# Three experts instead of two with fixed places in a decoder step's expert loop, and a new order of passes

## The chip, the cores and the metric

The kernel runs on one core of a Trainium2 chip. The metric is the device time of one execution in microseconds. TensorE (PE) multiplies, VectorE (DVE), ScalarE (ACT) and GpSimd (POOL) do the rest, and SyncE (SP) issues most of the transfers; all work from their own instruction queues and meet at semaphores. The core's transfers share 16 DMA engines.

## The reference, cut to what matters

One decoder layer for 512 prompt rows and 64 sample rows of width 1024, all in float32: a state space branch and an attention branch, merged and projected by `w_o`, then 16 experts of which each row uses two, then a gated embedding and a final norm. The change touches the experts and the loads around `w_o`:

```python
def hier_moe(h, w_rg, b_rg, w_re, b_re, w_gate, w_up, w_down):
    ...
        glog = (hf @ w_rg + b_rg).astype(f32)
        gsel = jnp.argmax(glog, axis=-1)
        ...
        top_v, top_i = lax.top_k(elog, TOP_K_INNER)
        wts = jax.nn.softmax(top_v, axis=-1) * gw
        eid = gsel[:, None] * EXPERTS_PER_GROUP + top_i
        comb = jnp.einsum('cke,ck->ce', jax.nn.one_hot(eid, N_EXPERTS, dtype=f32), wts)
        a = jnp.einsum('cd,edf->cef', hf, w_gate)
        b = jnp.einsum('cd,edf->cef', hf, w_up)
        act = jax.nn.silu(a) * b * comb[..., None].astype(hf.dtype)
        return jnp.einsum('cef,efd->cd', act, w_down)
...
        x = x + mix
        x = x + hier_moe(rms_norm(x, norm2_g[l]), ...)
        x = x + jax.nn.sigmoid(x @ w_ple_gate[l]) * (p_l @ w_ple[l])
```

The 576 rows make 1152 choices. A gate or up matrix of one expert is 1024 x 256 and a down matrix 256 x 1024, 1 MiB each, 48 MiB for all.

## The kernel before, in words

After the attention the two branches' products fill `merged`, and `w_o` (loaded as two halves, `wo0` for output columns 0 to 511 and `wo1` for 512 to 1023) multiplies it. `second_norm_steps` is the hand-written order of TensorE's steps from there: products with `w_o` ("m", pair of tiles, number), transposes ("xT"), router products ("rt", "rb"), and the products of the embedding ("pp"). `w_o_product` (L1640 on) says which half each product reads: the first, number 1 of pair 0, reads `wo0`. The last reader of `wo1` is product 7 of pair 1, the last of `wo0` is product 4 of pair 1, which comes later.

Then the experts are computed by gathered rows. A pass has 128 rows: rows of `h2_dram` (the normed rows, stored in five pieces) are gathered by a list, turned on TensorE, multiplied by gate and up (`gate_up`, L1766, or `gate_up_of_two`, L1779), activated, turned and multiplied by down (`down`, L1803, or `down_of_two`, L1812), and stored to `ye_dram`. TensorE's order in the loop (L1850 on) is gate and up of pass n, turn of pass n-1, rows of pass n+1, down of pass n-1.

An expert stands at one of 16 columns. The experts are sorted by their number of rows, and `RANK_OF_COLUMN` says which rank goes to which column. `COLUMNS_OF_PASS` says which columns a pass computes: a pass of one column has 128 slots for it, a pass of two gives 96 (or 64) to the first and 32 (or 64) to the second. Columns 12, 13 and 14 are small and are split over two neighbouring passes, so their weights stay for two passes. Experts 0 and 1 have columns 0 and 1 whatever their counts, so their weights can be loaded before the router is done. The rows of an expert that has more than its column's slots would be computed in a second round of the whole loop.

Weights are loaded in the order `LOADED`. Load number l of gate and up goes to slot l mod 4: slots 0 and 1 are `wgu`, slots 2 and 3 are ring buffers 1 and 2, in which before that the halves of `w_o` lie. Load number l of down goes to slot (l + 2) mod 3, of which two are in `merged`. On SyncE `gate_up_weights(l)` waits until the last pass that reads load l - 4 has done its gate and up products, and `down_weights(l)` until the last pass that reads the load before in the same slot has done its down products (`LAST_PASS`, `down_before`). SyncE does this in one fixed order, written out at L965 to L991. The gathers are issued by GpSimd and the stores by ScalarE, from queues of their own.

## Time and profile before

| | us |
|---|---|
| median of three runs | 799.75 |
| lowest and highest | 797.71, 799.83 |
| the profiled execution | 797.28 |
| its span | 795.5 |

Busy in that span: TensorE 762.2 us (96%), VectorE 379.9 (48%), ScalarE 204.9 (26%), GpSimd 106.8 (13%). The chain of work that ended last is TensorE for 80% of the span and DMA for 8%, and within the DMA part the loads of down matrices are the largest. The output projection runs from 485 to 550 us, the experts from 566 to 716, the gated embedding and the last norm from there to the end. The rows further down are of four kinds: windows (busy time of each engine in a stretch, then the granted clock, the busy share of the DMA engines and GB/s), waits (who waited for whom), the chain in order of time, and timelines of single engines.

### The profile page before, as it was taken

How to read it: one execution, taken by the hardware profiler on the slowest of the kernel's cores; microseconds unless marked ns; L12 is line 12 of the kernel's file. 1: busy time of each engine (PE TensorE's matmuls, PEld its weight loads, DVE VectorE, ACT ScalarE, POOL GpSimd, SP SyncE). 2: the span in 40 equal slices, each digit the busy share in tenths (PEclk: the TensorE clock that was granted, in tenths of full speed). 3: DMA queues.
4: the chain of work that ended last, by engine and by line, in shares of the span. 5: the costliest groups of instructions: out<-in, count | busy, mean ns of one | idle time of the engine just before them, and what ended most of it. 6: DMA issues, size and time to landing. Idle time of an engine off the chain costs nothing.

```text
span 795.5 us, 12983 instructions
## 1 busy us (share of the span) xinstructions
PE 762.2 (96%) x5070; PEld 494.9 (62%) x5070; DVE 379.9 (48%) x850; ACT 204.9 (26%) x485; POOL 106.8 (13%) x160
## 2 busy tenths in 40 slices
PE   8999999999999999889999999999999999998995
PEld 5455588777778788555566775445556564654442
DVE  3269523997232323766624378434732212214865
ACT  3011213112223354654523200134111111123223
POOL 3000006000000311334500100011111101015002
PEclk9999999999999999999999999999999999999998
DMA  9640493841440499200030279003799999996002
GB/s 324 160 126 0 112 278 139 99 133 57 140 97 17 139 233 266 94 1 1 1 120 2 96 216 384 1 14 128 282 407 409 416 418 416 417 373 211 17 14 106
DMA packets 81287, 136.50 MB, mean 172 GB/s; under 512 B 33926, under 2 KB 57546, under 8 KB 77010
## 3 DMA queue, kind: packets, MB, share of 16 engines
q1 hardware_dynamic: 64700, 110.17, 41.7%
q0 software_dynamic: 3728, 13.38, 4.9%
q10 hardware_dynamic: 12798, 12.12, 4.6%
q8 instruction: 41, 0.67, 0.3%
q14 instruction: 20, 0.16, 0.1%
HBM read 116.55 MB, written 21.19 MB: 173 GB/s over the span
## 4 chain that ended last, share of the span: by engine, by line
PE 80%; DMA 8%; DVE 6%; issue 2%; ACT 2%; POOL 1%; DVEq 0%; SPq 0%; POOLq 0%; ACTq 0%
PE ps L1215 29%; PE ps L1300 10%; PE ps L1656 6%; PE ps L1904 5%; PE ps L1788 4%; PE ps L1222 3%; PE ps L1776 3%; DMA merged<-in_w_exp_down 3%; DMA w_slot<-in_w_exp_down 2%; PE ps L1441 2%; PE ps L1820 2%; PE ps L1491 2%; PE ps L1537 2%; PE ps L1518 2%; DMA wgu<-expert_rows,pos_i 1%
## 5 line engine op out<-in xcount | busy, mean ns | idle before, releaser
L1215 PE MATMUL ps<-w_slot,hT 128*128 128x396 f32 (+1 forms) x192 | 71.1, 529 | 0.6 <-DMA w_slot<-in_w_in 0.4
L1215 PE MATMUL ps<-hT,w_slot 128*128 128x288 f32 x256 | 63.1, 407 | 0.0
L1215 PEld LDWEIGHTS ps<-hT,w_slot 128*128 128x128 f32 x256 | 48.3, 190 | 13.9 <-issue 0.8
L1215 PEld LDWEIGHTS ps<-w_slot,hT 128*128 128x128 f32 x192 | 36.1, 190 | 32.5 <-issue 13.4
L2987 DVE SCALAR_TENSOR_TENSOR th<-th,ps 128x256 f32<-128x256 f32 x12 | 5.1, 421 | 103.2 <-ACT th L2248 103.2
L1788 PE MATMUL ps<-w_slot,hT 128*32 128x256 f32 x544 | 49.7, 380 | 0.0
L1300 PE MATMUL ps<-hT,w_slot 128*128 128x288 f32 x144 | 37.3, 407 | 0.0
L1215 PE MATMUL ps<-qg,w_slot 128*128 128x288 f32 x128 | 33.7, 408 | 0.0
L1788 PEld LDWEIGHTS ps<-w_slot,hT 128*32 128x32 f32 x544 | 26.3, 110 | 10.0 <-issue 2.3
L2728 DVE TENSOR_REDUCE nm_p<-ps 128x2 f32<-128x256 f32 (+3 forms) x32 | 25.0, 819 | 15.6 <-PE ps L1491 15.5
L1300 PEld LDWEIGHTS ps<-hT,w_slot 128*128 128x128 f32 x144 | 27.3, 190 | 7.6 <-issue 0.2
L1088 POOL TENSOR_TENSOR hT<-hT,w_p 128x512 f32<-128x512 f32 (+3 forms) x11 | 25.1, 2284 | 50.6 <-DVE w_p L2360 50.6
L1215 PE MATMUL ps<-onsaT,w_slot 128*128 128x288 f32 x128 | 31.2, 406 | 0.0
L1776 PE MATMUL ps<-wgu,hT 128*128 128x256 f32 x128 | 28.9, 382 | 0.9 <-DVE hT L2360 0.9
L2148 ACT ACTIVATE hT<-ps,nm_p 128x128 f32<-128x128 f32 (+3 forms) x44 | 22.6, 524 | 26.1 <-DVE nm_p L2728 19.0
L1215 PEld LDWEIGHTS ps<-onsaT,w_slot 128*128 128x128 f32 x128 | 24.3, 190 | 6.7
L1788 PE MATMUL ps<-wgu,hT 128*32 128x256 f32 x352 | 28.3, 379 | 0.0
L1999 ACT ACTIVATE hT<-ps 128x512 f32<-128x512 f32 (+1 forms) x14 | 7.2, 553 | 81.8 <-PE ps L1699 71.0
L1776 PEld LDWEIGHTS ps<-wgu,hT 128*128 128x128 f32 x128 | 23.9, 190 | 6.7 <-issue 2.5
L2360 DVE TENSOR_TENSOR qg<-qg,ps 128x288 f32<-128x288 f32 x18 | 8.2, 455 | 39.6 <-PE ps L1300 39.5
L1215 PEld LDWEIGHTS ps<-qg,w_slot 128*128 128x128 f32 x128 | 23.2, 190 | 5.4
L1820 PE MATMUL ps<-merged,actT 128*32 128x512 f32 x160 | 25.4, 595 | 0.5 <-ACT actT L2252 0.5
(508 smaller groups left out, 1416.5 us busy)
## 6 DMA issues: line engine op xcount, KB each, us to landing
merged<-in_w_exp_down SPq DMA_DIRECT2D x10, 1024.0 KB, 15.9
w_slot<-in_w_in SPq DMA_DIRECT2D x8, 1024.0 KB, 7.7
wgu<-in_w_exp_gate SPq DMA_DIRECT2D x8, 1024.0 KB, 12.1
wgu<-in_w_exp_up SPq DMA_DIRECT2D x8, 1024.0 KB, 14.1
w_slot<-in_w_exp_gate SPq DMA_DIRECT2D x8, 1024.0 KB
w_slot<-in_w_exp_up SPq DMA_DIRECT2D x8, 1024.0 KB
w_slot<-in_w_exp_down SPq DMA_DIRECT2D x6, 1024.0 KB
expert_rows<-onsaT ACTq DMA_DIRECT2D x12, 512.0 KB, 8.2
```

Source lines behind the costliest of these rows:

```text
L1088: pool.tensor_tensor(p4, p4, w_p[:, i].rearrange("p a b -> p (a b)").unsqueeze(2).broadcast_to([P, 4, n]), ALU.mult).then_inc(pr_scaled, 1)
L1215: ins = pe.matmul(out, a, b, start=(n == 0), stop=(n == len(pairs) - 1))
L1222: ins = pe.matmul(out[64 * c:64 * c + 64, 0:n], a, b[c], start=(k == 0), stop=(k == len(pairs) - 1))
L1300: ins = pe.matmul(o[:, 0:HALF], weights[:, k], rows[:, k], start=(first and k == 0), stop=(k == 3), skip_group_check=True)
L1441: ins = pe.matmul(ps[:, 7, 0:NBLK], w1(k)[:, n], kvct[:, k, n % CS, n // CS:n // CS + NBLK], start=(n == 0), stop=(n == CL - 1))
L1656: ins = pe.matmul(o, rows[:, k], weights[:, k], start=(k == 0 and i in (1, 2, 5)), stop=(k == 3), skip_group_check=True)
L1776: ins = pe.matmul(ps[:, 2 + u, FF * w:FF * w + FF], hgT[:, u, k], w0[:, w, k], start=(k == 0), stop=(k == KD - 1))
L1788: ins = pe.matmul(ps[g:g + 32, 2 + u, FF * w:FF * w + FF], hgT[:, u, k, g:g + 32], gate_up_slot(l)[:, w, k], start=(k == 0), stop=(k == KD ...
L1820: ins = pe.matmul(ps[g:g + 32, 4 + c, :], actT[:, u, f, g:g + 32], down_slot(l)[:, f, 512 * c:512 * c + 512], start=(f == 0), stop=(f == 1))
L1904: ins = pe.matmul(o, rows[:, k], weights[:, k], start=(k == 0 and i in (1, 2, 5)), stop=(k == 3), skip_group_check=True)
L2148: ins = act.activation(probs[i % PBUFS][:, (2 * c + kh) * n:(2 * c + kh) * n + n], ps[:, 2 * (at % 2) + kh, 0:n], ACT.Exp, bias=nm_p[:, at ...
L2728: dve.tensor_reduce(nm_p[:, at], ps[:, 2 * (at % 2):2 * (at % 2) + 2, 0:n], axis=X, op=ALU.max, negate=True).then_inc(pr_max, 1)
```

## The change

Expert 2 gets a fixed column too. `RANK_OF_COLUMN`, `COLUMNS_OF_PASS` and `LOADED` are new: passes 0 to 2 compute experts 0, 1 and 2 alone, and the seven paired passes are 3, 4, 6, 7, 8, 9 and 10 (before 1, 2, 4, 5, 7, 8 and 10). The halves of `w_o` change ring buffers, so that `wo1`, which is done with first, lies where gate and up number 2 go; these two loads are issued right after router step ("rb", 1). SyncE's order in the loop is rewritten for the new passes.

```diff
+PINNED = 3
-COLUMNS_OF_PASS = [[0], [1, 12], [2, 12], [3], [4, 13], [5, 13], [6], [7, 14], [8, 14], [9], [10, 15], [11]]
+COLUMNS_OF_PASS = [[0], [1], [2], [3, 12], [4, 12], [5], [6, 13], [7, 13], [8, 15], [9, 14], [10, 14], [11]]
...
-LOADED = [0, 1, 12, 2, 3, 4, 13, 5, 6, 7, 14, 8, 9, 10, 15, 11]
+LOADED = [0, 1, 2, 3, 12, 4, 5, 6, 13, 7, 8, 15, 9, 14, 10, 11]
...
-           ("so", ("ab", KD - 1, 1)), ("no", ("bb", KD - 1, 1)), ("wo0", AFTER_W_O), ("wo1", AFTER_W_O),
+           ("so", ("ab", KD - 1, 1)), ("no", ("bb", KD - 1, 1)), ("wo1", AFTER_W_O), ("wo0", AFTER_W_O),
...
-            load_weights("wo0")
+            load_weights("wo1")
...
-            load_weights("wo1")
+            load_weights("wo0")
...
+            sp.wait_ge(pe_done, PLAN.done(("rb", 1)))
+            load_gate_up(2, 2)
             sp.wait_ge(pe_done, PLAN.done(AFTER_W_O))
             sp.wait_ge(h2_out[0], 16 * 3)
             sp.wait_ge(h2_out[1], 16 * 2)
             load_down(1, 1)
             sp.wait_ge(order_made, 1)
-            at_column = {0: 0, 1: 1}
+            at_column = {i: i for i in range(PINNED)}
...
-            for l in range(2, NX):
+            for l in range(PINNED, NX):
                 read_column(l)
                 load_gate_up(l, expert(l))
             load_down(2, expert(2))
...
                 gate_up_weights(5)
                 down_weights(3)
                 gate_up_weights(6)
+                down_weights(4)
                 gate_up_weights(7)
-                down_weights(4)
+                down_weights(5)
                 gate_up_weights(8)
-                down_weights(5)
+                gate_up_weights(9)
                 down_weights(6)
-                gate_up_weights(9)
+                gate_up_weights(10)
                 down_weights(7)
-                gate_up_weights(10)
+                down_weights(8)
                 gate_up_weights(11)
-                down_weights(8)
+                down_weights(9)
                 gate_up_weights(12)
-                down_weights(9)
+                gate_up_weights(13)
                 down_weights(10)
-                gate_up_weights(13)
-                down_weights(11)
                 gate_up_weights(14)
                 gate_up_weights(15)
+                down_weights(11)
                 down_weights(12)
...
-            for at, cap in ((slice(0, 1), 128), (slice(1, 3), 96), (slice(3, 4), 128), (slice(4, 6), 96), (slice(6, 7), 128),
-                            (slice(7, 9), 96), (slice(9, 10), 128), (slice(10, 11), 64), (slice(11, 12), 128), (slice(12, 16), 64)):
+            for at, cap in ((slice(0, 3), 128), (slice(3, 5), 96), (slice(5, 6), 128), (slice(6, 8), 96), (slice(8, 9), 64),
+                            (slice(9, 11), 96), (slice(11, 12), 128), (slice(12, 16), 64)):
                 pool.memset(cap_at[:, at], float(cap))
...
-            for e in range(2):
+            for e in range(PINNED):
                 pool.memset(first_at[:, e:e + 1], float(2 ** (21 - e)))
...
-                    pe.matmul(out[96:P, 1 + h:8 + h:3], ident[:, 32 * h:32 * h + 32], by_column[:, 12:15], start=True, stop=True)
-                return pe.matmul(out[64:P, 10:11], ident[:, 0:64], by_column[:, 15:16], start=True, stop=True)
+                    pe.matmul(out[96:P, 3 + h:10 + h:3], ident[:, 32 * h:32 * h + 32], by_column[:, 12:15], start=True, stop=True)
+                return pe.matmul(out[64:P, 8:9], ident[:, 0:64], by_column[:, 15:16], start=True, stop=True)
```

The slots of the columns change with it: 128 for columns 0, 1, 2 (fixed experts), 5 and 11, 64 for columns 8 and 12 to 15, 96 for the rest. The two busiest other experts have 128 slots, the third busiest 96.

SyncE's queue from the rows of the embedding to the first expert that the sort decides, before (`w_slot0` to `w_slot2` are the ring buffers, `kv`, `merged` and `wgu` hold what their sources say; `order_i` is the sorted list of experts):

```order
L923 DMA kv<-in_p_prompt 128x4x256 [waits merged_made,outputs_written]
L924 DMA kv<-in_p_sample 64x256
L751 DMA w_slot0<-in_w_ple 128x2x1024 [waits pe_done]
L918 DMA w_slot0<-in_w_exp_down 128x2x1024
L928 DMA kv<-in_final_norm_g 128x1024 [waits pe_done]
L918 DMA merged<-in_w_exp_down 128x2x1024 [waits h2_written1,h2_written0,pe_done]
L941 TENSOR_LOAD order_i [waits rows_gathered0,order_made]
L941 ISA x2
L914 ISA
L914 DMA w_slot1<-in_w_exp_gate 128x2048
L914 DMA w_slot1<-in_w_exp_up 128x2048
L941 TENSOR_LOAD order_i
```

and after:

```order
L929 DMA kv<-in_final_norm_g 128x1024 [waits pe_done]
L915 DMA w_slot1<-in_w_exp_gate 128x2048 [waits pe_done]
L915 DMA w_slot1<-in_w_exp_up 128x2048
L919 DMA merged<-in_w_exp_down 128x2x1024 [waits h2_written1,h2_written0,pe_done]
L944 TENSOR_LOAD order_i [waits rows_gathered0,order_made]
L944 ISA x2
L915 ISA
L915 DMA w_slot2<-in_w_exp_gate 128x2048
L915 DMA w_slot2<-in_w_exp_up 128x2048
L919 DMA merged<-in_w_exp_down 128x2x1024
```

The loads into `w_slot1` have moved ahead of the wait for the stores of the normed rows and of the wait for the sort.

SyncE's queue late in the expert loop, before, from down number 11 (to `merged`) over gate and up 14 and 15 (to `w_slot1` and `w_slot2`) to down number 12 (to `w_slot0`):

```order
L918 DMA merged<-in_w_exp_down 128x2x1024 [waits down_done]
L955 REGISTER_ALU
L914 ISA [waits gate_up_done]
L914 DMA w_slot1<-in_w_exp_gate 128x2048
L914 DMA w_slot1<-in_w_exp_up 128x2048
L914 ISA [waits gate_up_done]
L914 DMA w_slot2<-in_w_exp_gate 128x2048
L914 DMA w_slot2<-in_w_exp_up 128x2048
L960 REGISTER_ALU
L918 DMA w_slot0<-in_w_exp_down 128x2x1024 [waits down_done]
L960 REGISTER_ALU
```

and after, from down number 10 (to `merged`) over gate and up 14 and 15 to down numbers 11 and 12:

```order
L919 DMA merged<-in_w_exp_down 128x2x1024 [waits down_done]
L958 REGISTER_ALU
L915 ISA [waits gate_up_done]
L915 DMA w_slot1<-in_w_exp_gate 128x2048
L915 DMA w_slot1<-in_w_exp_up 128x2048
L915 ISA [waits gate_up_done]
L915 DMA w_slot2<-in_w_exp_gate 128x2048
L915 DMA w_slot2<-in_w_exp_up 128x2048
L963 REGISTER_ALU
L919 DMA merged<-in_w_exp_down 128x2x1024 [waits down_done]
L919 DMA w_slot0<-in_w_exp_down 128x2x1024 [waits down_done]
L963 REGISTER_ALU
```

Down number 11 has moved behind gate and up 14 and 15.

## Rows read from the trace of the kernel before

**Rows 1.** The page: busy time by engine, and TensorE's clock, DMA and GB/s in slices.

```profile
PE 762.2 (96%) x5070; PEld 494.9 (62%) x5070; DVE 379.9 (48%) x850; ACT 204.9 (26%) x485; POOL 106.8 (13%) x160
...
PEclk9999999999999999999999999999999999999998
```

**Rows 2.** The expert stage in one window: busy us per engine, clock, DMA share, GB/s.

```profile
600.00:700.00 100.00, 98.06 (x1028) 58.91 (x1017) 16.32 (x32) 15.71 (x34) 6.88 (x12) 1.00 1.02 415
```

**Rows 3.** TensorE's timeline, passes 1, 4, 6 and 7: start us, us, instruction, [idle before <-releaser].

```profile
577.69 0.42 PE L1788 MATMUL ps<-wgu,hT 128*32 128x256 f32 x3
...
624.62 7.11 PE L1788 MATMUL ps<-w_slot,hT 128*32 128x256 f32 x128
...
636.47 7.17 PE L1776 MATMUL ps<-wgu,hT 128*128 128x256 f32 x32
...
648.13 0.39 PE L1788 MATMUL ps<-wgu,hT 128*32 128x256 f32 x3
...
657.73 3.70 PE L1215 MATMUL ps<-merged,actT 128*128 128x512 f32 x8 [1.27 <-DMA merged<-in_w_exp_down]
```

**Rows 4.** TensorE's waits from 560 to 740: us in total, times, longest.

```profile
PE ps L1924 <- DVE x L2360: 2.0, 1, 2.0
...
PE ps L1820 <- DMA merged<-in_w_exp_down: 0.6, 1, 0.6
```

**Rows 5.** The chain that ended last, in order of time: start us, us, what.

```profile
649.05 21.17 DMA merged<-in_w_exp_down
...
674.09 19.80 DMA w_slot<-in_w_exp_down
693.94 3.71 PE ps L1215 x8
...
698.30 7.17 DMA expert_rows<-onsaT
...
707.58 10.33 DMA wgu<-expert_rows,pos_i
...
720.20 1.25 PE ps L1924 x8
```

**Rows 6.** The issues of down loads (L918): issue to landing.

```profile
DMA to landing us min/median/max: 4.9/15.9/21.2
```

**Rows 7.** The second half of W_o: its landing, its issue, and TensorE's first product.

```profile
w_slot<-in_w_o SPq DMA_DIRECT2D x1, 2048.0 KB, 8.7
...
471.22 0.43 SPq L751 DMA_DIRECT2D w_slot<-in_w_o  x1
...
485.13 3.60 PE L1656 MATMUL ps<-w_slot,merged 128*128 128x512 f32 x8
```

**Rows 8.** Around the router: TensorE, a window, SyncE and GpSimd.

```profile
543.93 0.29 PE L1718 MATMUL ps<-groups_sum,actT 128*128 128x20 f32 x2
...
543.00:552.00 9.00, 8.67 (x62) 5.26 (x64) 3.95 (x8) 4.96 (x7) 1.84 (x5) 1.00 0.15 61
...
557.62 0.37 SPq L918 DMA_DIRECT2D merged<-in_w_exp_down  x1
...
546.73 0.61 POOL L1123 DMA_DIRECT2D h_rows<-hn  x1
...
560.89 1.06 POOL L1137 DMA_INDIRECT hT<-h_rows,idx  x1 [5.67 <-DVE idx L2360]
```

**Rows 9.** SyncE's waits around the router.

```profile
SPq L931 <- DMA h_rows<-hn: 17.1, 1, 17.1
```

**Rows 10.** TensorE's last product and windows of the end, columns as in rows 2.

```profile
782.02 3.60 PE L1904 MATMUL ps<-merged,hT 128*128 128x512 f32 x8
...
788.00:790.00 2.00, 0.00 (x0) 0.00 (x0) 1.97 (x3) 1.13 (x4) 0.20 (x1) 1.00 0.00 0
790.00:792.00 2.00, 0.00 (x0) 0.00 (x0) 1.00 (x2) 0.12 (x2) 1.15 (x3) 0.56 0.30 123
792.00:794.00 2.00, 0.00 (x0) 0.00 (x0) 0.97 (x2) 0.00 (x0) 0.00 (x0) 0.50 0.76 294
```

More of the change, by code:

```diff
@@ L61 @@
 MAXR = -(-ROWS // CAP)
-RANK_OF_COLUMN = [0, 1, 6, 2, 7, 8, 3, 9, 10, 4, 14, 5, 11, 12, 13, 15]
-COLUMNS_OF_PASS = [[0], [1, 12], [2, 12], [3], [4, 13], [5, 13], [6], [7, 14], [8, 14], [9], [10, 15], [11]]
+PINNED = 3
+RANK_OF_COLUMN = [0, 1, 2, 5, 6, 3, 7, 8, 14, 9, 10, 4, 11, 12, 13, 15]
+COLUMNS_OF_PASS = [[0], [1], [2], [3, 12], [4, 12], [5], [6, 13], [7, 13], [8, 15], [9, 14], [10, 14], [11]]
 NPASS = len(COLUMNS_OF_PASS)
 OF_PARITY = [-(-NPASS // 2), NPASS // 2]
-LOADED = [0, 1, 12, 2, 3, 4, 13, 5, 6, 7, 14, 8, 9, 10, 15, 11]
+LOADED = [0, 1, 2, 3, 12, 4, 5, 6, 13, 7, 8, 15, 9, 14, 10, 11]
 LAST_PASS = [max(n for n, columns in enumerate(COLUMNS_OF_PASS) if column in columns) for column in LOADED]
@@ L1102, in _ @@
             row_of(base_at[:, 0:NPASS], 0, CAP)
-            row_of(base_at[:, 12:15], CAP + 96, 3 * CAP)
-            pool.memset(base_at[:, 15:16], float(10 * CAP + 64))
-            for at, cap in ((slice(0, 1), 128), (slice(1, 3), 96), (slice(3, 4), 128), (slice(4, 6), 96), (slice(6, 7), 128),
-                            (slice(7, 9), 96), (slice(9, 10), 128), (slice(10, 11), 64), (slice(11, 12), 128), (slice(12, 16), 64)):
+            row_of(base_at[:, 12:15], 3 * CAP + 96, 3 * CAP)
+            pool.memset(base_at[:, 15:16], float(8 * CAP + 64))
+            for at, cap in ((slice(0, 3), 128), (slice(3, 5), 96), (slice(5, 6), 128), (slice(6, 8), 96), (slice(8, 9), 64),
+                            (slice(9, 11), 96), (slice(11, 12), 128), (slice(12, 16), 64)):
                 pool.memset(cap_at[:, at], float(cap))
@@ L1109, in _ @@
                 pool.memset(split_at[:, at], float(split))
-            for e in range(2):
+            for e in range(PINNED):
                 pool.memset(first_at[:, e:e + 1], float(2 ** (21 - e)))
-            row_of(first_at[:, 2:NE], NE - 3, -1)
-            for at in (slice(0, 2), slice(2, 3), slice(3, 4), slice(4, 6), slice(6, 7), slice(7, 9), slice(9, 10), slice(10, 11),
-                       slice(11, 12), slice(12, 15), slice(15, 16)):
+            row_of(first_at[:, PINNED:NE], NE - 1 - PINNED, -1)
+            for at in (slice(0, 3), slice(3, 5), slice(5, 6), slice(6, 8), slice(8, 9), slice(9, 11), slice(11, 12), slice(12, 15), slice(15, 16)):
                 row_of(rank_of[:, at], RANK_OF_COLUMN[at.start], 1)
```

## The prediction, made before the changed kernel ran

> **What bounds the kernel now.** I read the page's slices first, then the expert stage in windows, then who waits for whom, then the chain. TensorE has work in 96% of the span and its clock is granted in full until the last slice [rows 1]. So a change gains only where TensorE stands still, and loses wherever it makes it stand. In the expert stage (566 to 716 us) two things run side by side at nearly the same pace. From 600 to 700 us 415 GB/s move and the 16 DMA engines are full (share 1.02) [rows 2]. TensorE takes 11.74 us a pass: gate and up of pass 1 begin at 577.69, of pass 7 at 648.13, six passes later [rows 3]. A paired pass costs what a single one does (7.11 against 7.17 us for gate and up, 3.7 for down) [rows 3], so the new order of passes changes none of TensorE's own work: seven passes are paired before and after. TensorE waits for weights three times only: 1.27 us, 0.55 us and some 0.1 us, 1.9 us in all, each time for a down projection [rows 3, 4, 5]. The reader is to see in the chain how they come about: a down load issued at 649.05 lands 21.17 us later, one issued at 674.09 lands 19.80 us later, because all SyncE loads stand in one line [rows 5]. Unloaded, the same load lands in 4.9 us [rows 6]. So the margin of a load is the time from its issue to its use, and its issue is bound to the pass that frees its slot.
>
> **Part by part.**
>
> *W_o halves swapped.* The half that TensorE reads first (columns 0 to 511) now comes second. The second half is issued at 471.22 and takes 8.7 us [rows 7], so it is there at 479.9. Its first reader is the product at 485.13 [rows 7]: 5 us to spare, cost 0. Without that cover the whole projection would slip by what is missing.
>
> *Expert 2's gate and up (two loads, 2 MiB) behind the router product of tile 1.* The slot of the old second half is free once that product's row (TensorE, 543.93) is done. 2 MiB are 2.1 MB, 5.1 us at 415 GB/s; from 543 to 552 the engines move 61 GB/s, so there is room [rows 8]. Queued behind it on SyncE are the wait for the five stores of normed rows (17.1 us) and behind it the down load at 557.62 [rows 8, 9], 13 us later: free. Beside it runs the store issued at 546.73, which may land some 2 us late; the first gather at 560.89 waits for the list of rows, not for it [rows 8]. Cost 0 to 1 us, 0 taken. A load that had stood at 566.18, 2 MiB or 5.1 us of the line, is gone from the full stretch.
>
> *What the early load is worth.* At most the 1.9 us of waits: TensorE has no other wait for weights.
>
> *Tables.* GpSimd runs three small table writes fewer, on an engine that is ahead at this point. 0.
>
> *The order of passes.* This is the term that counts. A load of gate and up needs the slot of the load four before it, a down load that of three before it. I wrote down for each load the pass that frees its slot and the pass that reads it. Before, every down load has two passes between (slot free after down of pass n, read by down of pass n+2). After, two have one: number 11 (column 15, read in pass 8) takes the slot of number 8 (column 13), whose last reader is now pass 7; number 13 (column 14, read in pass 9) takes the slot of column 8, read in pass 8. Number 11 can be issued only when down of pass 7 ends, and down of pass 8 starts 11.74 - 3.5 = 8.2 us later, where the landings of before are 16 to 21 us. In front of it in the line stand gate and up 14 and 15, released together by gate and up of pass 8.
>
> Its landing: in the new order TensorE takes one expert a pass in passes 0 to 2, so loads run at one slot a pass and the line runs empty. Per pass 3 MiB of weights, 0.5 MiB gathered and 0.5 MiB written are 4.2 MB, 10.1 us of 11.74. It is empty for the last time when gate and up of pass 4 end, at 577.69 + 3 x 11.74 + 7.1 = 620.0, where two loads are released at once. From there to the end of number 11: gate and up of eight experts (8 to 15, 2 MiB each), six downs (6 to 11, 1 MiB), five gathers and five stores of 0.5 MiB, 27 MiB = 28.3 MB. At 415 GB/s [rows 2] that is 68.2 us. With 2.4 us from the last byte's turn to the landing (4.9 us [rows 6] less 2.5 us of transfer) it lands at 620.3 + 68.2 + 2.4 = 690.9, the 0.3 being SyncE's own step. The same count made for before, from 566.2 to number 12 (48.5 MiB, 122.5 us), gives 691.1 where the trace has 693.89 [rows 5]; scaled to 68 us that adds 1.5. I take 691.6, between. Down of pass 8 would start at 577.69 + 8 x 11.74 + 7.1 + 1.3 = 680.0. TensorE slips by 11.6 us, about 2 of them already in front of gate and up of pass 9 (number 13 of those, counted likewise, lands near 673.5, wanted at 671.6), the rest in front of down of pass 8. Against the 1.9 us of before: **+9.7 us**. Least case: only gate and up 14 and 15, the down and 1 MiB of row traffic stand in the line from 667.6 on, 6.3 MB or 15.2 us plus 2.4: 685.2, a slip of 5.2, +3.3 net. Most: an effective 405 GB/s, 693.5, +11.6 net.
>
> Number 13 is issued when down of pass 8 ends, near 695.2, into an empty line, lands by 700 to 703 and is wanted at 703.6: 0.
>
> *The clock.* TensorE stands still for 9 to 10 us there. The trace has one such stretch, its end: the last products start at 782.02 and end by 785.6; the clock is granted in full up to 790, 0.56 from 790 to 792 and 0.50 from there, the lower level of 1.2 GHz [rows 10]. So it falls within the stall. No row shows it coming back; the cost lies between 0 and a whole down at half speed, 3.5 us. I take the middle, **+1.7 us**.
> The Trainium skill (TensorE: Matmul & The Clock Gate, Part 1, on the HAM clock gate) says that the clock stays at the lower level at first when work resumes. By it the term is above zero; without any such effect the sum below would be 1.7 us less.
>
> *The tail.* Before, the store of pass 9's rows takes 7.17 us and the gather behind it 10.33 us, TensorE waits 2.0 us for tile 0 and starts at 720.20 [rows 4, 5]. In the new order the stall has let the line run down, so both land some 3 us earlier against TensorE, and the products that cover them end at 718.2: **-2.0 us** (0 to -2).
>
> Sum: +9.7 + 1.7 - 2.0 = **+9.4 us**. On the profiled run (797.28 us, span 795.5) 806.7; on the median of the runs, 799.75, 809.2. The profiled run is at the low end of the runs (797.71 to 799.83), so I take a value between, 808.5.
>
> **Rivals.**
> *A shorter stall.* If less stands in the line than I count, the net slip is 3.3 to 7 us, the clock stays or costs little, the tail gives 2: 801 to 805. For it: the line runs empty earlier. Against it: the same count fits before within 2.6 us.
> *No stall, the purpose reached.* The 1.9 us of waits and the 2.0 us of the tail go: 799.75 - 3.9 = 795.9. It needs number 11 to land within 8.2 us with 4 MiB in front of it; the smallest landing of an unloaded 1 MiB is 4.9 us, and 4 MiB are 10 us more.
> *A longer one.* The clock costs its full 3.5, number 13 comes late as well by 2 to 4 us, the tail gives nothing: 813 to 818.
> *A second round.* The fixed experts have 128 slots each, but the third busiest of the rest now has 96 instead of 128. Counting the router's choices on the reference's inputs (seed 0) gives 82, 80 and 100 rows for experts 0 to 2 and 113, 111, 90, 86, 69 and less for the rest: all fit, one round. With 97 rows in one place the whole loop would run again, some 12 x 11.74 = 141 us more.
>
> **How the numbers follow.** The forecast 0.74, a shorter stall 0.12, no stall 0.05, a longer one 0.08, a second round 0.01. The range of 802.5 to 814 holds the forecast with its bounds (net slip 7 to 11.6, clock 0 to 3.5, tail 0 to -2, on either base) and half of its two neighbours. About 0.3%, 2.4 us, is what a measurement of this kernel can tell from no change. Slower by more than that: 0.89; within it 0.06 (the lower edge of the short stall, a little of no stall); faster 0.05.
>
> **What would show it.** A wait of 8 to 10 us in front of the paired down product, between 680 and 693, for a down load whose slot is an expert's, and 1 to 3 us in front of gate and up one pass earlier; a granted clock below 1.00 there; idle DMA time between 575 and 620 where there was none; the loads of expert 2 between 544 and 552 and the first pass still at 569.7. I am wrong if that load lands before 684, if the line is not served in order, or if the first pass starts later than 571.

## The result, and the profile after

| | before | after |
|---|---|---|
| median, us | 798.88 (4 runs) | 809.46 (4 runs) |
| lowest and highest | 797.71, 799.83 | 808.96, 811.46 |
| the profiled execution, its span | 797.28, 795.5 | 809.38, 807.6 |

The ratio is 1.0138, 95% interval 1.0111 to 1.0165: slower by 10.6 us, inside the range and 1 us over the forecast. Medians and ratios in this document are of the fast runs, which leaves out one run of two_first_pg0 (1587 us) and three of the kernel before beside the experiments.

In the changed kernel all line numbers are two or three higher: `gate_up` is L1778, `gate_up_of_two` L1790, `down_of_two` L1822, the loads of gate and up L915, of down L919. TensorE's waits from 560 to 760 us, which answer to [rows 4]:

```profile
PE ps L1822 <- issue: 8.1, 1, 8.1
PE ps L1790 <- DMA wgu<-in_w_exp_up: 3.5, 1, 3.5
PE ps L1790 <- DMA w_slot<-in_w_exp_up: 1.2, 1, 1.2
```

Three waits in a row, 12.8 us, where there were three of 1.9 us together. The trace puts the longest down to "issue", that is, to nothing it can name; the place and the landing below tell what it is. TensorE's timeline around it (start us, us, instruction, [idle before <-releaser]), which answers to [rows 3]:

```profile
661.24 7.11 PE L1790 MATMUL ps<-w_slot,hT 128*32 128x256 f32 x128 [1.19 <-DMA w_slot<-in_w_exp_up]
...
676.68 7.59 PE L1790 MATMUL ps<-wgu,hT 128*32 128x256 f32 x128 [3.52 <-DMA wgu<-in_w_exp_up]
684.48 1.04 PE L1761 MATMUL ps<-ident,hT 128*128 128x128 f32 x8
693.58 6.30 PE L1822 MATMUL ps<-merged,actT 128*32 128x512 f32 x32 [8.06 <-issue]
...
719.59 3.64 PE L1822 MATMUL ps<-merged,actT 128*32 128x512 f32 x32 [0.46 <-ACT actT L2254]
```

The rows are gate and up of pass 8, gate and up of pass 9, the turn of the rows, down of pass 8, and down of pass 10, the last paired one. The down product of pass 8 waits 8.06 us, and its 32 matmuls then take 6.30 us where those of pass 10 take 3.64. SyncE's issues in the same stretch, for what it waited for:

```profile
668.61 0.33 SPq L915 DMA_DIRECT2D w_slot<-in_w_exp_gate  x1
669.04 0.38 SPq L915 DMA_DIRECT2D w_slot<-in_w_exp_up  x1
669.67 0.33 SPq L915 DMA_DIRECT2D w_slot<-in_w_exp_gate  x1
670.10 0.39 SPq L915 DMA_DIRECT2D w_slot<-in_w_exp_up  x1
673.34 0.38 SPq L919 DMA_DIRECT2D merged<-in_w_exp_down  x1
673.91 0.38 SPq L919 DMA_DIRECT2D w_slot<-in_w_exp_down  x1
700.05 0.92 SPq L919 DMA_DIRECT2D merged<-in_w_exp_down  x2
```

and, for the load issued at 673.34, its size and its time to landing:

```profile
merged<-in_w_exp_down SPq DMA_DIRECT2D x1, 1024.0 KB, 20.1
```

Down load 11 goes out at 673.34, behind 4 MiB, and is wanted at 685.52. It lands at about 693.5, and TensorE starts at 693.58: the same kind of landing as the 19.8 and 21.2 us of [rows 5], on a load that now has one pass of room and not two. After 673.91 nothing is issued for 26 us, because every further load waits for a product that waits for this one. Windows (busy us per engine, granted clock, DMA share, GB/s) show how much the line carries, and the clock:

```profile
580.00:600.00 20.00, 20.00 (x91) 15.35 (x90) 7.25 (x30) 2.93 (x7) 2.29 (x4) 1.00 0.97 366
600.00:620.00 20.00, 20.00 (x278) 10.84 (x276) 2.04 (x4) 2.62 (x6) 1.14 (x2) 1.00 1.00 361
620.00:640.00 20.00, 20.00 (x188) 12.39 (x188) 4.08 (x8) 3.71 (x8) 2.28 (x4) 1.00 1.00 391
...
688.00:690.00 2.00, 0.00 (x0) 0.00 (x0) 0.00 (x0) 0.00 (x0) 0.00 (x0) 0.68 0.99 401
690.00:692.00 2.00, 0.00 (x0) 0.00 (x0) 0.00 (x0) 0.00 (x0) 0.00 (x0) 0.50 1.03 414
...
696.00:698.00 2.00, 2.00 (x16) 0.65 (x12) 0.00 (x0) 0.60 (x1) 0.00 (x0) 0.50 0.00 0
698.00:700.00 2.00, 2.00 (x24) 0.65 (x19) 0.00 (x0) 0.07 (x1) 0.00 (x0) 0.76 0.00 0
700.00:702.00 2.00, 2.00 (x44) 1.26 (x40) 0.00 (x0) 0.53 (x1) 0.00 (x0) 1.00 0.42 37
```

The clock falls during the wait, stands at 0.50 (1.2 GHz) when work comes back at 693.6, and is full (2.4 GHz) again only from some point between 698 and 700. From 696 to 700 us nothing at all moves.

**Where the 12.1 us between the two spans are.** The times of a stretch have to be counted from a mark, since each execution loses a different amount before the experts: the first gate product starts at 569.71 in the trace of before and here at

```profile
570.34 5.45 PE L1778 MATMUL ps<-wgu,hT 128*128 128x256 f32 x24 [0.89 <-DVE hT L2362]
```

That +0.6 is already there at the first product of `w_o` (485.13 [rows 7] against 485.76), ahead of the experts; up to there the change has only exchanged the two loads of `w_o`, for which nothing waits. Pass 7 starts its gate product at 648.12 against 648.13 [rows 3], so the passes up to there took 0.6 us less. Then: waits 12.8 against 1.9, +10.9; gate of pass 9 in 7.59 and not 7.11 us, and down of pass 8 in 6.30 and not 3.64, both at a lower clock, +3.1. The tail, from the down product of pass 10 to the first transpose of x, is 705.43 to 720.20 before and 719.59 to 732.34 after, -2.0. Sum: 0.6 - 0.6 + 10.9 + 3.1 - 2.0 = 12.0.

### The profile page after: what moved, and what is told of

Read it like the earlier page. It is cut to its first block, busy times and chain, and to the rows that moved or that the text cites. A ratio compares the mean times of both kernels' runs of the same rounds, so it can differ in the third digit from the quotient of the medians.

```text
span 807.6 us, 12971 instructions
## 1 busy us (share of the span) xinstructions
PE 766.4 (95%) x5070; PEld 497.5 (62%) x5070; DVE 379.9 (47%) x850; ACT 204.6 (25%) x485; POOL 106.0 (13%) x157
## 4 chain that ended last, share of the span: by engine, by line
PE 84%; DVE 5%; DMA 4%; issue 3%; ACT 2%; POOL 1%; SPq 0%; DVEq 0%; POOLq 0%; ACTq 0%
PE ps L1217 29%; PE ps L1302 10%; PE ps L1658 6%; PE ps L1790 5%; PE ps L1906 5%; PE ps L1778 4%; PE ps L1224 3%; PE ps L1822 3%; DMA wgu<-in_w_exp_up 2%; PE ps L1443 2%; PE ps L1493 2%; PE ps L1539 2%; PE ps L1520 2%; DMA w_slot<-in_w_in 1%; PE ps L1761 1%
## 5 line engine op out<-in xcount | busy, mean ns | idle before, releaser
L1790 PE MATMUL ps<-wgu,hT 128*32 128x256 f32 x480 | 43.1, 380 | 3.5 <-DMA wgu<-in_w_exp_up 3.5
L1822 PE MATMUL ps<-merged,actT 128*32 128x512 f32 x152 | 28.1, 672 | 8.5 <-issue 8.1
L1790 PEld LDWEIGHTS ps<-wgu,hT 128*32 128x32 f32 x480 | 22.9, 110 | 13.9 <-issue 6.3
L1790 PE MATMUL ps<-w_slot,hT 128*32 128x256 f32 x416 | 28.4, 379 | 1.2 <-DMA w_slot<-in_w_exp_up 1.2
L2262 ACT ACTIVATE onsaT<-ps 128x512 f32<-128x512 f32 x24 | 14.3, 597 | 48.0 <-PE ps L1822 32.1
L2254 ACT ACTIVATE actT<-ps 128x256 f32<-128x256 f32 x12 | 4.6, 383 | 80.8 <-PE ps L1797 80.8
## 6 DMA issues: line engine op xcount, KB each, us to landing
w_slot<-in_w_exp_up SPq DMA_DIRECT2D x8, 1024.0 KB, 13.3
w_slot<-in_w_exp_down SPq DMA_DIRECT2D x6, 1024.0 KB, 13.5
```

What stands on the lines that cost most here:

```text
L1790: ins = pe.matmul(ps[g:g + 32, 2 + u, FF * w:FF * w + FF], hgT[:, u, k, g:g + 32], gate_up_slot(l)[:, w, k], start=(k == 0), stop=(k == KD ...
L1822: ins = pe.matmul(ps[g:g + 32, 4 + c, :], actT[:, u, f, g:g + 32], down_slot(l)[:, f, 512 * c:512 * c + 512], start=(f == 0), stop=(f == 1))
```

## The experiments

The theory: what costs is the order of passes and of SyncE's line, through loads whose buffer comes free one pass before they are read. The early load of a third expert costs nothing and gains nothing. The rivals: the early load and the exchanged halves of `w_o` cost something themselves; or passes of one expert in front leave the line late as a whole, wherever its loads stand. The table has each kernel with the stretch of its trace from the start of the first gate product to the first transpose of x (before: 569.71 to 720.20); the ratio is to the kernel before, run beside it on the same chip. The chips differ between groups of experiments, so kernels of different groups are compared by their ratios.

| kernel | median us (runs) | ratio, 95% interval | stretch |
|---|---|---|---|
| before | 798.88 (4) | | 150.5 |
| after | 809.46 (4) | 1.0138 (1.0111 to 1.0165) | 162.0 |
| order_alone | 808.98 (4) | 1.0138 (1.0112 to 1.0164) | 160.9 |
| early_alone | 800.76 (12) | 1.0019 (1.0001 to 1.0037) | 152.0 |
| down11_first | 803.17 (8) | 1.0054 (1.0033 to 1.0075) | 154.2 |
| own_slot | 803.76 (5) | 1.0050 (1.0026 to 1.0073) | 154.7 |
| clock_kept | 808.01 (4) | 1.0113 (1.0082 to 1.0144) | 161.3 |
| col15_late | 810.39 (4) | 1.0146 (1.0117 to 1.0174) | 164.3 |
| col15_pg0 | 805.16 (4) | 1.0080 (1.0051 to 1.0109) | 159.8 |
| two_first | 804.44 (6) | 1.0073 (1.0047 to 1.0100) | 154.4 |
| two_first_pg0 | 799.00 (11) | 1.0012 (0.9992 to 1.0032) | 151.9 |
| two_first_late | 799.61 (12) | 1.0016 (0.9997 to 1.0036) | 151.3 |

### The two halves of the change, apart

**order_alone** puts the early load back behind the first gather.

```diff
-            sp.wait_ge(pe_done, PLAN.done(("rb", 1)))
-            load_gate_up(2, 2)
...
             sp.wait_ge(hg_ld[0], 16)
+            load_gate_up(2, 2)
             for l in range(PINNED, NX):
```

> The new order of passes without the early load: gate and up of expert 2 are issued where the first sorted expert's are (after the rows of pass 0 have landed), all else as in the changed kernel. If the order of passes makes the loss (the line of loads runs empty early, down 11 is issued late), nothing changes: 809.5 us, within 1 us, waits of TensorE for weights of some 12.8 us in passes 8 and 9. If the 2 MiB beside the router's work cost something (late stores of normed rows, late first gather), this kernel is faster than the changed one by 2 us or more.

It measures 808.98 us, the time of the changed kernel. Its waits are 0.9, 3.5 and 6.8 us, 11.2 against 12.8. Two products behind the waits lose 3.8 us by the clock (8.80 us for gate of pass 9, 5.76 for down of pass 8), against 3.1 in the changed kernel. The order carries the whole loss, and the early load has made the waits no shorter.

**early_alone** is the kernel before with the early load and nothing of the new passes. Expert 3 gets the third fixed place, column 2, and the halves of `w_o` are exchanged (the tables and that exchange are left out of the cut below).

```diff
-LOADED = [0, 1, 12, 2, 3, 4, 13, 5, 6, 7, 14, 8, 9, 10, 15, 11]
+LOADED = [0, 1, 2, 12, 3, 4, 13, 5, 6, 7, 14, 8, 9, 10, 15, 11]
...
+            sp.wait_ge(pe_done, PLAN.done(("rb", 1)))
+            load_gate_up(2, 3)
```

> The early load without the new order: the passes of the kernel before, with expert 3 (66 rows, so that it fits 96 slots) fixed in column 2, its gate and up loaded behind the router product of tile 1, W_o halves swapped. If the order is the cause, this is at least as fast as the kernel before: the 1.9 us of waits for down weights shrink to 1.0 or less and 0 to 1 us comes from the tail, 796 to 798.5 us. If the early load itself costs, it is slower than before, 801 us or more.

800.76 us falls between the two expectations, so it supports neither, and the interval is just clear of 1. The trace says why it is no clean test of the early load. TensorE's timeline has a wait that neither kernel had, before down of pass 1:

```profile
603.09 0.63 PE L1824 MATMUL ps<-merged,actT 128*32 128x512 f32 x3 [3.22 <-issue]
```

and SyncE's has the load that it is for:

```profile
591.76 0.38 SPq L918 DMA_DIRECT2D w_slot<-in_w_exp_down  x1
```

To load the fixed expert early I had to exchange two entries of `LOADED`. With that, the down matrix of column 12, read in pass 1, became load 3 and takes the buffer that down of pass 0 frees: one pass of room again, issued 591.76, used 603.09, 11.3 us later. The experiment has the fault of the new order in a second place, with a wait of 3.2 us. The early load itself is tested cleanly by order_alone, and by the last experiment.

### What stands ahead of down load 11

**down11_first** moves one line of SyncE's order.

```diff
                 down_weights(10)
+                down_weights(11)
                 gate_up_weights(14)
                 gate_up_weights(15)
-                down_weights(11)
                 down_weights(12)
```

> One line moved: SyncE issues down 11 before gate and up 14 and 15 instead of after. Theory 1 (what stands in front of down 11 in the line makes the long stall): down of pass 8 waits no more, a wait of 3 to 4 us appears in front of down of pass 9 for down 13, the one of 3.5 us in front of gate and up of pass 9 stays; waits 7 to 8 us instead of 12.8, the clock does not fall (3 us), 800.5 to 802.5 us. Theory 2 (the bytes missed while the line was empty must be caught up in any order): the stall only changes its place, 806 to 809 us.

**own_slot** gives load 11 a buffer that nothing else uses by then (`hn`), so that it need not wait at all, and issues it at the same place in SyncE's order.

```diff
         def down_slot(l):
+            if l == 11:
+                return hn[:]
...
                 down_weights(10)
+                load_down(11, expert(11))
                 gate_up_weights(14)
                 gate_up_weights(15)
-                down_weights(11)
```

> Down 11 gets a slot of its own (the buffer of the normed rows, free in this stage) and is issued before gate and up 14 and 15 without waiting for down of pass 7. If only the 4 MiB in front of it matter, the same as with the line moved, within 1 us: 800.5 to 802.5. If the late release of the slot matters besides, it is faster than that kernel by 2 us or more. By theory 2 it stays at 806 to 809.

803.17 and 803.76 us: some 6 us of the 10.6 are gone in both. That is 0.7 and 1.3 us above the 802.5 that the first theory allowed, and far below the 806 of the second. The free buffer adds nothing. So what hurt load 11 was the 4 MiB in front of it. In down11_first it still waits for down of pass 7, goes out at 675.85, and down of pass 8 starts 12.1 us later without a wait:

```profile
675.85 0.38 SPq L919 DMA_DIRECT2D merged<-in_w_exp_down  x1
...
687.98 2.35 PE L1822 MATMUL ps<-merged,actT 128*32 128x512 f32 x20
```

In both traces the 8 us wait is gone, and what is left is 1.1 (own_slot 1.4) us and 3.5 us for gate and up of passes 8 and 9, and a new one for down load 13, from the chain of down11_first (start us, us, what):

```profile
659.61 19.38 DMA wgu<-in_w_exp_up
...
691.80 10.44 DMA merged<-in_w_exp_down
702.25 0.04 issue
702.29 3.69 PE ps L1822 x32
```

The first row is gate and up load 13, which pass 9 waits for, the second down load 13. Load 13 is the other down load with a single pass of room. In the changed kernel it was covered by the emptied line (no wait at 708.02); with load 11 on time it waits 2.5 us. Neither kernel comes back to the time of before: 7.1 and 6.7 us of waits are left where that one has 1.9.

The waits for gate and up have a place in the order too. Counting in `LOADED` and `COLUMNS_OF_PASS` as the prediction does for the down loads, gate and up 11, 12 and 13 are read three passes after the one that frees their slot in the kernel before, and two passes after it in the new order. Every kernel with the new order waits 0.9 to 1.8 us for number 11, and those in which number 13 has two passes wait 3.1 to 3.6 us for it. In col15_late, further down, number 13 has three again and nothing waits for it. But number 14 has two passes in the kernel before as well, without a wait, and no run changed this alone: it is a count that fits and not a cause shown.

### The clock

**clock_kept** gives TensorE something to do during the 8 us.

```diff
             def down_of_two(j, n, u):
+                if n == 8:
+                    for _ in range(64):
+                        pe.transpose(ps[:, 7, 256:384], ident[:], ident[:])
                 down_there(j, n)
```

> The changed kernel, with 64 transposes of the 128x128 identity into an unused part of ps put on TensorE in front of the wait of the down product of pass 8 (they take about 64 x 0.11 = 7 us of the 8.06 us for which TensorE stands there); nothing is left out. Theory: TensorE's granted clock falls because the engine stands, so with work in the wait the 32 matmuls of the down product take 3.6 us again and not 6.3: 809.5 - 2.7 = 806.8 us (805.8 to 807.8), with the same landing of the down load. Rival: the clock follows something else (the transfers, the load of the whole chip), the product stays at 6.3 us, and the time is that of the changed kernel, 809.5 us (808.5 to 810.5), or longer if the transposes push the product back.

TensorE's timeline, with gate and up of pass 9, the transposes and down of pass 8:

```profile
676.42 8.43 PE L1790 MATMUL ps<-wgu,hT 128*32 128x256 f32 x128 [3.07 <-DMA wgu<-in_w_exp_up]
...
685.93 7.15 PE L1818 MATMUL ps<-ident 128*128 128x128 f32 x64
693.60 3.64 PE L1825 MATMUL ps<-merged,actT 128*32 128x512 f32 x32 [0.52 <-issue]
```

and a window from inside the transposes:

```profile
688.00:690.00 2.00, 2.00 (x21) 2.00 (x20) 0.02 (x1) 0.00 (x0) 0.00 (x0) 1.00 1.00 401
```

The clock is granted in full and the product takes 3.64 us again, not 6.30, while the DMA engines move as much as in the changed kernel (401 GB/s in these two microseconds in both): the clock had fallen because TensorE stood, and its price in that product was 2.7 us. The Trainium skill (TensorE: Matmul & The Clock Gate, Part 1) has the array at half of its clock by default after idling and at the full one when busy; the trace agrees, 0.50 against 1.00. The time, 808.01 us, falls by less than the product does, 1.45 us against 2.7. It lies between the two expectations (805.8 to 807.8, and 808.5 up), and its interval overlaps that of the changed kernel. The trace says where the rest went, for its stretch is only 0.7 us shorter. The waits up to gate of pass 9 are 1.1 us longer in all (0.92 before down of pass 7, 1.80 and not 1.19 before gate of pass 8, 3.07 and not 3.52 before gate of pass 9), the transposes and the wait behind them take 0.4 us less than the wait of 8.06, gate of pass 9 takes 8.43 us and not 7.59, and the first transpose of x waits 0.5 us for its gathers. Most of that lies ahead of the transposes and is none of their doing. So the 2.7 us in the product are shown, and a gain in the total is not.

### Another place for the last paired column

**col15_late** exchanges columns 14 and 15: 14 in passes 8 and 9, 15 in pass 10. SyncE issues gate and up 15 behind down 12, so that one expert's gate and up, not two, stand ahead of down load 11, which is now that of column 14 (the tables are left out of the cut).

```diff
-COLUMNS_OF_PASS = [... [7, 13], [8, 15], [9, 14], [10, 14], [11]]
+COLUMNS_OF_PASS = [... [7, 13], [8, 14], [9, 14], [10, 15], [11]]
-LOADED = [0, 1, 2, 3, 12, 4, 5, 6, 13, 7, 8, 15, 9, 14, 10, 11]
+LOADED = [0, 1, 2, 3, 12, 4, 5, 6, 13, 7, 8, 14, 9, 10, 15, 11]
...
                 gate_up_weights(14)
-                gate_up_weights(15)
                 down_weights(11)
                 down_weights(12)
+                gate_up_weights(15)
```

> The changed kernel with columns 14 and 15 exchanged in the order: 14 in passes 8 and 9, 15 in pass 10 (before: 15 in pass 8, 14 in passes 9 and 10), so that only one expert's gate and up weights, not two, stand in SyncE's line ahead of the down load that pass 8 wants. Theory (the order of the line and the time at which buffers come free set the waits): bytes carried through at the 405 GB/s of the stretch give no wait for gate and up of pass 9, and one of about 6.6 us for the down load of pass 8, against 12.8 us of waits in the changed kernel; 809.5 - 6.2 = 803.3, less up to 1.5 us of clock: 802 to 804. Rival (the line is late as a whole because the passes of one expert stand first, whatever its order is): the waits stay at 11 to 13 us in some other place, 807.5 to 810.

810.39 us: the theory missed by 6 us, and the time is 0.4 us above the rival's range. The trace shows what both had. The wait that I had worked out is there, 7.3 us against 6.6, and the clock takes 2.8 us behind it (6.46 us for the product), where I had allowed up to 1.5. But there is a second wait, 4.6 us, that the arithmetic did not have, and the clock takes some 2 us behind that one too: the first four matmuls of the last down product take 3.78 us, the next four 1.72. With the 1.5 us for gate and up of pass 8 the waits are 13.3 us. The chain, with an issue of SyncE in the middle:

```profile
680.40 7.26 issue
687.66 6.46 PE ps L1824 x32
...
706.59 0.38 SPq L752 DMA_DIRECT2D w_slot<-in_w_ple_gate  x1
...
707.15 16.07 DMA w_slot<-in_w_exp_down
...
723.27 3.78 PE ps L1218 x4
...
728.21 1.72 PE ps L1218 x4
```

Down load 14 now waits until down of pass 9 has ended (705.9), and SyncE stands at it with `pg0` (2 MiB, `in_w_ple_gate`) behind it, which need not wait for that. The last down load, released by the same product, comes behind `pg0`: issued at 707.15, used at 723.27.

**two_first** asks the rival's question directly: only two passes of one expert in front, the others spread. The fixed expert is number 3, and `LOADED`, the tables and SyncE's order, which are left out of the cut, follow the new passes.

```diff
-COLUMNS_OF_PASS = [[0], [1], [2], [3, 12], [4, 12], [5], [6, 13], [7, 13], [8, 15], [9, 14], [10, 14], [11]]
+COLUMNS_OF_PASS = [[0], [1], [2, 12], [3, 12], [4], [5, 13], [6, 13], [7], [8, 14], [9, 14], [10, 15], [11]]
```

> The early load of a third expert kept, but only two passes of one expert in front, and the others spread: passes [0], [1], [2,12], [3,12], [4], [5,13], [6,13], [7], [8,14], [9,14], [10,15], [11]; the expert with the fixed place is number 3 and not 2. Nothing is left out. Theory (a load waits for its buffer, and what counts is how many passes lie between the release and the use): bytes carried through at 405 GB/s give waits of 1.7 and 0.5 us, 2.2 in all, as against 12.8 in the changed kernel and 1.9 in the one before: 799 to 801 us, and at best 797.5 if the third expert's early load takes up these. Rival (any order that puts single passes first leaves the line behind for good): 803 us or more, as in the two kernels in which the down load was moved ahead.

804.44 us, again the rival's number, though the profiled execution, 800.65, is the fastest of the six. And again the waits that I had worked out are nearly right (1.5 and 0.6 us against 1.7 and 0.5), and a third of 4.3 us stands before the last down product, which loses 1.7 us by the clock besides (3.38 us for its first four matmuls, 1.72 for the next). TensorE's timeline, two issues of SyncE and a window:

```profile
714.41 3.38 PE L1219 MATMUL ps<-w_slot,actT 128*128 128x512 f32 x4 [4.28 <-DMA w_slot<-in_w_exp_down]
...
698.02 0.48 SPq L751 DMA_DIRECT2D w_slot<-in_w_ple_gate  x1
698.69 0.44 SPq L918 DMA_DIRECT2D w_slot<-in_w_exp_down  x1
...
696.00:698.00 2.00, 2.00 (x16) 0.85 (x9) 0.00 (x0) 0.81 (x2) 0.00 (x0) 1.00 0.04 8
```

From 696 to 698 us the DMA engines move 8 GB/s, while `pg0`, whose slot is free since the gate product of pass 10 (692.5), waits in the queue behind a load that has to wait. That can be tested.

**two_first_pg0** and **col15_pg0** move `pg0` ahead of that load.

```diff
+                sp.wait_ge(g_done, j * NPASS + (NPASS - 1))
+                sp.sem_inc(slot_free, 1)
+                load_weights("pg0")
                 down_weights(14)
-                sp.wait_ge(g_done, j * NPASS + (NPASS - 1))
-                sp.sem_inc(slot_free, 1)
-                load_weights("pg0")
```

> The kernel with two single passes in front, with one thing moved: SyncE issues the first of the two ple_gate loads (pg0, 2 MiB) ahead of the down load at position 14 and no longer behind it. In two_first that down load waits for its buffer until the down product of pass 9 has ended (697.4 us), pg0 and the last down load stand behind it, the DMA engines are idle from 690 to 697, and TensorE stands 4.3 us for the last down load (issued 698.7, landed 714.4). Theory (this one wait behind a wait is what the arithmetic had left out): pg0 goes out at about 692.5 into the idle stretch, the last down load lands by 706, 4.3 us of waiting go, and from the end of the gate product of pass 11 to the first transpose of x it is 13.6 to 15.7 us as in the changed kernel and the one before, and not 19.4: 804.4 - 3.8 to 5.8 = 798.6 to 800.6. Rival (the order with single passes first leaves the whole line late, and the loads merely change places): the last wait comes back elsewhere, 803 to 805.

> The kernel with columns 14 and 15 exchanged, with pg0 ahead of the down load at position 14, as in two_first_pg0. In col15_late that down load waits until the down product of pass 10's predecessor has ended (705.9 us), the last one is issued at 707.15 and lands at 723.2, and TensorE stands 4.6 us for it. Theory: those 4.6 us go and the stretch from the end of the gate product of pass 11 to the first transpose of x falls from 20.4 to 13.6 to 15.7 us; the 7.3 us in front of the down product of pass 8 and the clock that they cost stay: 810.4 - 4.7 to 6.8 = 803.6 to 805.7. Rival (whole line late): 808 to 811.

799.00 and 805.16 us: both inside what the theory expected, and outside what the rival did. In two_first_pg0 `pg0` goes out at 693.57, the last down load at 698.99, and the wait before the last down product is gone. A smaller one is there instead, before down of pass 10, for down load 14, which now stands behind `pg0` (0.8 us in col15_pg0):

```profile
693.57 0.39 SPq L751 DMA_DIRECT2D w_slot<-in_w_ple_gate  x1
698.44 0.37 SPq L918 DMA_DIRECT2D merged<-in_w_exp_down  x1
698.99 0.37 SPq L918 DMA_DIRECT2D w_slot<-in_w_exp_down  x1
...
707.42 3.64 PE L1824 MATMUL ps<-merged,actT 128*32 128x512 f32 x32 [1.63 <-DMA merged<-in_w_exp_down]
```

So the second wait was a position in SyncE's queue, not a debt of the single passes in front: while SyncE stands at one load, it issues nothing that comes after. The gain is 4.9 us by the two ratios (1.0073 and 1.0012) and 5.3 for columns 14 and 15. The two stretches of two_first and two_first_pg0 differ by only 2.5 us, because the second trace also has a wait of 2.3 us for a down load at 668.6, ahead of everything that was moved, which the first has not: such waits of 1 to 2 us differ between executions of one order. The Trainium skill (DMA: Bandwidth & Descriptors, the section on queues, rings and completion order) says that each DMA engine takes the descriptors of one ring in their order. The trace agrees with it: in two_first the last down load, 1 MiB right behind the 2 MiB of `pg0`, is used 15.7 us after its issue, where the fastest down load of the kernel before lands in 4.9 [rows 6].

**two_first_late** puts the early load of two_first_pg0 back to its old place.

```diff
-            sp.wait_ge(pe_done, PLAN.done(("rb", 1)))
-            load_gate_up(2, 3)
...
             sp.wait_ge(hg_ld[0], 16)
+            load_gate_up(2, 3)
```

> two_first_pg0 with its early load put back: gate and up of the third fixed expert are issued behind the first gather, as in the kernel before, and not behind the router product. Theory (what sets the waits is how late a buffer comes free, and the line has caught up by 620 us either way): the same time as two_first_pg0, 799.5 us (798 to 801), with the same waits of 1.5 us for gate and up of pass 7 or 8 and of 1 to 2 us for downs. Rival (the 2 MiB taken out of the full stretch are worth their 5.1 us of transfer, less what stands idle): 802 to 805 us, with waits in front of pass 2 or 3 that two_first_pg0 does not have.

799.61 against 799.00 us, or 1.0016 against 1.0012 by the ratios, and no wait for weights before 665 us in either. The early load is worth nothing that can be measured here, even in an order that wastes little of it. Two windows show where its 2 MiB go, first of two_first_pg0 and then of two_first_late:

```profile
580.00:600.00 20.00, 20.00 (x195) 11.96 (x197) 5.30 (x13) 3.70 (x8) 2.28 (x4) 1.00 0.96 359
```

```profile
580.00:600.00 20.00, 20.00 (x186) 12.98 (x185) 7.10 (x29) 2.83 (x7) 2.28 (x4) 1.00 1.02 416
```

With the early load the line carries 359 GB/s in the first passes, without it 416, and from 600 us on the two are equal (371 and 374). Buffers come free at TensorE's pace, so a load fetched ahead of time only makes the line slack afterwards.

None of these kernels beats the one before. The best two are within 0.2% of it, with intervals that hold 1. Their traces have 6.0 and 4.6 us of waits for weights against its 1.9, and a tail (down of pass 10 to the first transpose of x) of 12.6 and 13.5 us against its 14.8.

## Why the prediction was right, step by step

- **The order of passes.** Right in mechanism and place: down load 11, one pass of room, 4 MiB in front. It landed at 693.5 where I had 691.6 and was wanted at 685.5 where I had 682 (680.0 and the 2 us in front of pass 9). own_slot and down11_first show that the 4 MiB are what counts.
- **The waits, +9.7.** Measured +10.9. Three were there, not two. A wait of 1.19 us for gate and up load 11 before pass 8 was missing from my list, and that before pass 9 was 3.5 us and not 2. I had counted one load to its landing (691.6) and one more (673.5 for gate and up 13, measured 676.5), and listed the passes of room for the down loads alone; gate and up 11 to 13 had lost one as well.
- **The rate.** Taking 415 GB/s for the whole way was the smaller error. From 620 us, where the count begins, to 640 the engines moved 391 GB/s, with a share of 1.00. The bare count gave a landing of 690.9, with the whole of the 1.5 us that it was short on the kernel before 692.4, measured 693.5; I had taken 691.6.
- **The bounds.** Three of them do not follow from their own terms. At 405 GB/s the count gives a landing of 692.6 and a net of +10.7, not 693.5 and +11.6; the measured +10.9 lies above the first and below the second. The least case starts at 667.0 (577.69 + 7 x 11.74 + 7.1), not 667.6. And net 11.6 with 3.5 of clock on the higher base make 814.9, not 814. None of them moves the forecast.
- **"Its clock is granted in full until the last slice".** Misread: a 9 in the row of [rows 1] is 90% or more. The same trace has 0.94 from 360 to 390 us, and in it a fall and a return: 0.54 from 360 to 362, 0.61 to 364 and 1.00 from there (last section). So the end of the kernel was not the only such stretch, and a row for the clock's return was there to read when the clock term was set.
- **"Idle DMA time between 575 and 620".** Wrong as I had put it: the share there is 0.97 and 1.00. What falls is GB/s, from 405 and 412 to 366 and 361. The first of these falls belongs to the early load and not to the order: order_alone moves 415 GB/s from 580 to 600 us, and 376 in the next 20.
- **Load 13, 0.** Right in the changed kernel. down11_first and own_slot show that this was so only because the stall had emptied the line (2.5 and 1.3 us).
- **The clock, +1.7.** The term that was mis-sized: 3.1 us. The bounds of 0 and 3.5 held, though order_alone has 3.8, and the middle, a choice without a row behind it, was too low. The down product alone lost 2.7 us, as clock_kept shows, and the gate product behind the shorter wait 0.5. In order_alone these are 2.1 and 1.7.
- **The tail, -2.0.** Right in size, half right in its reason. ScalarE's store of the rows is no faster (issued 712.28, GpSimd goes on at 720.00: 7.7 us, against 7.4 from 698.30 to 705.68 before); only the gather behind it is, 8.1 us against 10.3.
- **The early load, the exchanged halves of `w_o` and the tables, 0.** Right: order_alone and two_first_late for the early load. The halves and the tables were never put back alone; for them there is only that the first product of `w_o` starts without a wait (485.76) and that the first gate product follows it as closely as before (84.6 us later in both). The cost that I named is seen, since the slowest store of normed rows lands in 7.0 us (4.1 before) and the down load behind SyncE's wait goes out at 559.81, 2.2 us later than before. No engine that sets the end waits for them.
- **The rival of a shorter stall, 801 to 805,** is what the kernel gives when one line of SyncE's order is moved: 803.2.

Being within 1 us was in part luck. Between the two profiled executions the sum was +9.4 and the measured difference +12.1, 2.7 us more. The forecast was near because it was read on a higher base (808.5 is 11.2 above the profiled execution of before), which had to do with the scatter of the runs and not with the loads.

## What to carry to other kernels

For weights that stream through a ring, write down for every load the step that frees its buffer and the step that reads it, and what stands between it and the head of the line. In this kernel a load with 4 MiB in front of it needed some 20 us, nearly two passes. Loads with one pass of room were late behind a full line (by 8.1, 7.3, 3.2 and 2.5 us in four kernels) and in time where the line was empty or nothing was released just ahead of them (load 13 of the changed kernel, load 11 of down11_first). Fetching more ahead of time is worth nothing where the next loads are bound to buffers that come free later. And look at each wait of the issuing queue for what is held up behind it that need not wait: moving one 2 MiB load past such a wait was worth 5 us in two kernels.

## What the runs showed that I had not expected

- The busy share of the DMA engines does not say how much they move. From 600 to 620 us the share is 1.00 at 361 GB/s in the changed kernel and 1.02 at 412 in the one before, whose row is

```profile
600.00:620.00 20.00, 20.00 (x219) 12.44 (x208) 2.04 (x4) 2.73 (x6) 1.15 (x2) 1.00 1.02 412
```

- The clock comes back late: work resumed at 693.58, the clock was still at 0.50 until 698, and full from 700. For 4 to 6 us the work took about twice as long.
- The clock also falls behind short waits, and the same waits do not always cost it. In the attention of the kernel before, from 354 to 360 us, TensorE has work for 3.4 of the 6 us; its waits there are 0.99, 0.51 and 1.08 us, none longer. Two windows of the kernel before, and the same two of two_first_pg0:

```profile
358.00:360.00 2.00, 0.95 (x6) 0.61 (x8) 0.76 (x4) 0.42 (x1) 1.09 (x1) 1.00 0.00 0
360.00:362.00 2.00, 2.00 (x9) 0.91 (x6) 1.54 (x2) 0.00 (x0) 1.66 (x1) 0.54 0.00 0
...
358.00:360.00 2.00, 0.94 (x6) 0.61 (x8) 0.77 (x4) 0.42 (x1) 1.08 (x1) 1.00 0.00 0
360.00:362.00 2.00, 2.00 (x16) 1.25 (x14) 1.76 (x3) 0.54 (x2) 1.67 (x1) 1.00 0.00 0
```

  TensorE did the same work up to 360 us, and then the clock was at 0.54 in the first and full in the second. It falls there in eleven of the twelve traces, between 355 and 370 us; the window from 360 to 390 has 0.94 in the kernel before and 0.90 in early_alone. The first product of `w_o` starts between 483.6 and 488.4 us, though TensorE's work ahead of it is the same, and the earliest start is that of two_first_pg0. Four traces have a second fall, near 322 us or near 10, and three of them have the latest starts (487.2 to 488.4). So the clock probably makes a good part of the scatter of some 5 us between runs of one kernel, which one trace for each kernel cannot show; it is why stretches were measured here from a mark behind it. Why the same waits cost the clock in one execution and not in another stays open.
